# Prompt attention of an encoder step: the head outputs' squares on ScalarE instead of GpSimd, each head's store and every second copy of weights issued earlier

## The reference, cut to what matters

```python
def diff_attn_prompt(q, k, v, lam):          # q, k: (1, 1024, 8, 2, 64), v: (1, 1024, 8, 128)
    for i in range(T // Q_BLOCK):            # blocks of 128 queries
        qs, qe = i * Q_BLOCK, (i + 1) * Q_BLOCK
        s = jnp.einsum('bqhcd,bkhcd->bhcqk', q[:, qs:qe], k[:, :qe])
        mask = chunk_id[None, :qe] <= chunk_id[qs:qe, None]
        p = jax.nn.softmax(jnp.where(mask, s, -jnp.inf), axis=-1)
        a = p[:, :, 0] - lam * p[:, :, 1]
        outs.append(jnp.einsum('bhqk,bkhv->bqhv', a, v[:, :qe]))

def diff_output(o, g_norm, lambda_init, w_o):
    o = rms_norm(o, g_norm) * (1.0 - lambda_init)     # per head, over its 128 columns
    return o.reshape(B, T, DIFF_V) @ w_o
```

## Time and profile before

| what | value |
|---|---|
| median of 3 runs | 2890.35 us (2889.14 to 2894.65) |
| the profiled execution | 2889.26 us, its span 2886.80 us |
| PE / DVE / ACT / POOL busy in the span | 2791.4 / 1168.9 / 866.4 / 1236.5 us |
| prompt attention within the span | about 1680 to 1892 us |
| mean granted clock of PE over the span | 0.989 |

### The profile page before, as it was taken

How to read it: one execution, slowest core, us unless ns; L and a number is a source line. 1 busy time by engine, 2 the same in 40 slices (tenths; PEclk the granted TensorE clock), 3 DMA queues, 4 the chain that set the end, 5 groups by cost and what they waited for, 6 DMA issues and landing times.

```text
span 2886.8 us, 39210 instructions
## 1 busy us (share of the span) xinstructions
PE 2791.4 (97%) x15484; PEld 2420.7 (84%) x15484; DVE 1168.9 (40%) x2079; ACT 866.4 (30%) x1513; POOL 1236.5 (43%) x654
## 2 busy tenths in 40 slices
PE   7999999999999999999999988899999999999997
PEld 7977757799889988997788867777798899989986
DVE  2153156452322233246544178855463322232245
ACT  2053242231222223222211056653141222222221
POOL 1211210343776567634212122133252775677645
PEclk9999999999999999999999999999999999999999
DMA  4111216110210221031444333476111201221021
GB/s 134 52 37 44 91 64 226 37 52 30 59 36 22 58 58 44 15 95 37 128 135 143 123 134 107 168 291 236 44 53 36 55 8 54 58 58 31 27 73 66
DMA packets 197372, 232.26 MB, mean 80 GB/s; under 512 B 8944, under 2 KB 141808, under 8 KB 195200
## 3 DMA queue, kind: packets, MB, share of 16 engines
q1 hardware_dynamic: 197248, 230.54, 24.8%
HBM read 184.90 MB, written 45.61 MB: 80 GB/s over the span
## 4 chain that ended last, share of the span: by engine, by line
PE 44%; DVE 4%; issue 1%; DMA 1%; ACT 1%; POOL 0%; SPq 0%; DVEq 0%; ACTq 0%
PE ps L1480 13%; PE ps L1498 12%; PE ps L1781 8%; PE ps L1668 3%; DVE stats L2513 1%; PE ps L1884 1%; PE ps L1751 1%; PE ps L1847 1%; PE ps L1918 1%; DMA o_scr<-oraw 1%; PE ps L1871 1%; PE ps L1470 1%; DVE stats L2226 1%; PE ps L1962 1%; ACT PR L1360 0%
## 5 line engine op out<-in xcount | busy, mean ns | idle before, releaser
L1480 PE MATMUL ps<-xt,wsplit 128*128 128x384 f32 x5184 | 908.2, 335 | 13.1 <-DVEq L2253 5.0
L1480 PEld LDWEIGHTS ps<-xt,wsplit 128*128 128x128 f32 x5184 | 900.8, 188 | 17.9 <-issue 7.1
L852 POOL TENSOR_TENSOR wsplit<-raw,wsplit 128x1024 fp32r<-128x1024 f32 x144 | 354.7, 2470 | 920.8 <-ACT wsplit L1072 843.1
L1498 PE MATMUL ps<-wsplit,xt 128*128 128x512 f32 x3024 | 707.0, 393 | 0.0
L1498 PEld LDWEIGHTS ps<-wsplit,xt 128*128 128x128 f32 x3024 | 564.8, 189 | 122.0 <-issue 6.5
L1781 PE MATMUL ps<-wsplit,HF 128*128 128x512 f32 x2016 | 468.6, 390 | 0.0
L1781 PEld LDWEIGHTS ps<-wsplit,HF 128*128 128x128 f32 x2016 | 377.3, 188 | 81.6 <-DVE x_res L2359 4.2
L2359 DVE TENSOR_TENSOR x_res<-x_res,ps 128x1024 f32<-128x1024 f32 x168 | 205.2, 1221 | 308.3 <-PE ps L1781 308.3
L2351 DVE TENSOR_SCALAR Hf<-ps 128x384 f32<-128x384 f32 x144 | 80.3, 558 | 499.1 <-PE ps L1480 498.4
L1278 ACT ACTIVATE Hf<-Hf 128x384 f32<-128x384 f32 x144 | 75.9, 527 | 428.1 <-DVE Hf L2351 428.1
L922 POOL TENSOR_TENSOR wsplit<-raw,wsplit 128x1024 fp32r<-128x1024 f32 x36 | 86.0, 2389 | 263.9 <-ACT wsplit L1255 263.9
(11 more groups left out here) (196 smaller groups left out, 2782.8 us busy)
## 6 DMA issues: line engine op xcount, KB each, us to landing
raw<-in_w_up SPq DMA_DIRECT2D x64, 512.0 KB, 5.5
raw<-in_w_down SPq DMA_DIRECT2D x64, 512.0 KB, 3.7
kq_scr<-kqst SPq DMA_DIRECT2D x64, 256.0 KB, 2.8
Kc<-in_cache_k SPq DMA_DIRECT2D x8, 2048.0 KB, 13.3
Vc<-in_cache_v SPq DMA_DIRECT2D x8, 2048.0 KB, 8.8
raw<-in_w_in_a SPq DMA_DIRECT2D x24, 512.0 KB, 3.7
out<-kvs SPq DMA_DIRECT2D x36, 256.0 KB, 2.2
raw<-in_w_kv SPq DMA_DIRECT2D x16, 512.0 KB, 4.4
```

Source lines behind the costliest of these rows:

```text
L852: nc.gpsimd.tensor_tensor(wsplit[:, slot, 1, :], raw[:, slot, :], wsplit[:, slot, 0, :].bitcast(F32), ALU.subtract).then_inc(lo_done, 1)
L1480: last = nc.tensor.matmul(ps[0:M, b, 0:GW], st, xt[:, c, k, ng * GW:(ng + 1) * GW], start=(k == 0 and i == 0), stop=(k == KT - 1 and i == 2))
L1498: last = nc.tensor.matmul(ps[:, u % 6, :], xt[:, a, 2 * j + k, tok:tok + P], wsplit[:, (g + j) % 4, c, k * 512:(k + 1) * 512], start=(j == ...
```

## The change

Four edits. ACT squares each head output in the step after its copy: one activation Square of 128x128 with its accumulator, which writes the sum of the row to `ssA` (`output_squares`); it stands after the second exponential of the loop's turn. POOL's `head_squares` is gone; its remaining waits on it are waits on ACT's count. SP issues `head_out(k - 1)` at step 4 of head k, ahead of that step's `head`, and no longer at step 7 behind `values_in`. DVE copies the far weights (`rest_weights`) ahead of `balance` instead of behind it.

```diff
@@ SP: the loop over the steps
         for s in range(STEPS):
+            if s % PT == 4 and s // PT:
+                head_out(s // PT - 1)
             if s % PT == 4 and s // PT + 2 < H_B:
                 head(s // PT + 2)
             if s % PT == PT - 1 and s // PT + 3 < H_B:
                 values_in(s // PT + 3)
-            if s % PT == PT - 1 and s // PT:
-                head_out(s // PT - 1)
@@ POOL
-        def head_squares(h):
-
-            pool.wait_ge(o_free, PT * (h + 1))
-            tt(osq[:], oraw[h % 2][:], oraw[h % 2][:], ALU.mult).then_inc(heads_squared, 1)
-            pool.wait_ge(heads_squared, h + 1)
-            for k, half in enumerate((64, 32, 16, 8, 4, 2, 1)):
-                to = osq[:, :, 0:half] if half > 1 else ssA[:, PT * h:PT * (h + 1)].unsqueeze(2)
-                tt(to, osq[:, :, 0:half], osq[:, :, half:2 * half], ALU.add).then_inc(heads_summed, 1)
-                pool.wait_ge(heads_summed, 7 * h + k + 1)
-
         for j in range(4):
             split_lo(G_O2 + j)
-        for h in range(H_B - 1):
-            head_squares(h)
+        pool.wait_ge(heads_squared, PT * (H_B - 1))
...
-        head_squares(H_B - 1)
+        pool.wait_ge(heads_squared, STEPS)
         nc.gpsimd.memset(Vc[:, 1, 4, :], 0.0).then_inc(smp_v_zero, 1)
@@ ACT
             if s % PT == 0 and h >= 2:
                 act.wait_ge(o_out[h % 2], 16 * (h // 2))
-                act.wait_ge(heads_squared, h - 1)
             nc.scalar.activation(oraw[h % 2][:, i, :], ps[:, 7, 0:P], ACT.Copy).then_inc(o_free, 1)
+
+        def output_squares(s):
+            h, i = step_of(s)
+            act.wait_ge(o_free, s + 1)
+            if s:
+                act.wait_ge(heads_squared, s)
+            nc.scalar.activation(osq[:, 0, :], oraw[h % 2][:, i, :], ACT.Square,
+                                 accum_out=ssA[:, step_index(s):step_index(s) + 1]).then_inc(heads_squared, 1)
...
             if s + 1 < STEPS:
                 exponentials(s + 1, 1)
+            if 0 <= s - 3:
+                output_squares(s - 3)
@@ DVE
             if s + 1 < STEPS:
                 maxima(s + 1)
-            if 0 <= s < STEPS:
-                balance(s)
             if 0 <= s - 1 and s % 2 == 1:
                 rest_weights(s - 1)
             if 0 <= s < STEPS:
+                balance(s)
                 combine(s)
...
-            dve.wait_ge(heads_summed, 7 * H_B)
+            dve.wait_ge(heads_squared, STEPS)
```

More of the change, by code:

```diff
@@ L307, in encoder_step @@
     heads_squared = sem("heads_squared")
-    heads_summed = sem("heads_summed")
     factor_made = sem("factor_made")
```

## The result

The changed kernel took 2870.41 us (median of 4 runs, 2868.65 to 2872.81) against 2889.74 us, ratio 0.9931 with a 95% interval of 0.9914 to 0.9948: 19.3 us less, where 2869 us, or 21.4 us less than the first median, was forecast. The profiled execution took 2868.72 us, its span 2866.6.

The account below looks back on a forecast made before the run. PE and DVE were taken to share the bound in an undisturbed prompt-attention head, with late stores stalling later heads. -18.6 + 0 - 2.4 = -21.0 us took the profiled 2889.26 to 2868.3, so 2869 us was forecast, range 2862 to 2881.

Parts of the forecast that it names:

- Stores sooner: Prompt attention, SP's queue: earlier head stores end ACT's wait at oraw and the lower clock, -18.6 us.
- Squares on ACT: Prompt attention, 64 steps: a 0.31 us square each fits ACT's idle time ahead of lead copies; 0, up to +5 us.
- upper bound of 5 us: Squares on ACT: cost if the 0.31 us slip stayed in two of eight steps a head, 16 x 0.31.
- POOL off and far weights sooner: Prompt attention, DVE: POOL's squares leave, far copy precedes balance; -2.4 us net, from -8 to +4.
- POOL's 0.59 us a head: DVE's factor product and combination, stretched beside POOL, shorten once POOL's squares leave; 4.7 us in eight heads.
- DVE's new wait: DVE would idle 0.6 us at the early far copy for PE's far transposes; with combination lags, up to 1.1 us a head.
- The seam to the sample stage: Second load of cached values loses its 1.9 us wait for POOL's zeroing, but off the chain: 0.
- (a): DVE becomes the bound in order, far copies waiting for PE in all 32 odd steps: +23.4 us, 2895 us; chance 0.06.
- (b): ACT becomes the bound, all 64 squares on the path: +19.8 us, 2889 us, no change; chance 0.06.
- (c): The wait only moves to another late thing at a head's start; half of 18.6 us comes back, 2881 us; chance 0.06.
- (d): PE becomes the only bound, every head falling to its 21.95 us: 2863 us; chance 0.12.
- The sum: Whole kernel: -18.6 + 0 - 2.4 = -21.0 us, giving 2868.3 us for the profiled execution, 2869 us forecast.

Follow-up runs that it names:

- e1: Kernel before with only the stores early (each head's store issued at step 4 of the next head): 2873.4 us, ratio 0.9945.
- e4: Changed kernel with the stores put back late, behind the values load at each head's last step: 2886.2 us, ratio to before 0.9987.
- e5: Changed kernel with every square done twice on ACT, the second into spare columns: 2868.1 us (one run).
- e6: Changed kernel with no squares of prompt head outputs on any engine, their sums set to one: 2873.5 us (one run).
- e2: Changed kernel with the copy of the far weights put back behind balance on DVE: 2872.8 us.
- e3: Changed kernel with the squares and sums back on POOL and none on ACT, stores and far copy as changed: 2875.2 us.
- e7: Changed kernel with balance ahead of the far copy again in one odd step of each head: 2869.1 us, ratio to before 0.9939.
- e8: e7 with the maxima of both maps as one reduction instead of two in a head's four small steps: 2868.6 us, ratio to before 0.9938.
- e10: Changed kernel with one more small DVE instruction, a second reciprocal, in every step: 2876.1 us (one run).

## Why the prediction was right, point by point

- **Stores sooner, -18.6 us: right.** e1 gives 18.63 us over the six heads from this edit alone. The reading that named the cause was the code's wait beside ACT's unexplained idle time, and e4's trace names the store outright. Taking the price from the periods and not from ACT's 15.6 us of idle time was right as well. But the working put the difference of 3 us down to the clock alone, and that it is so small is luck: a stall without the echo costs some 0.6 us less than ACT's idle time and one with it 0.9 us more (the last section has the rows), so that by an estimate from these the echo made some 6 of the 18.6 us. (The stall at 1770.30 us, whose windows show, is the second, not the third.)
- **Squares on ACT, 0: right**, and with more room than I saw. The square takes 0.32 us, and e5 and e6 leave the head where it is. The upper bound of 5 us is excluded. The sign given for it, that the idle time ahead of the lead copies falls by about 20 us, came true (21.6 us), but only some 12 us of that are the squares.
- **POOL off and far weights sooner, -2.4 us net: right in the sum, wrong in its parts.** Six heads gained 137.93 - 135.60 = 2.3 us here, 0.39 a head, where 0.3 was taken. But the working added POOL's 0.59 us a head, the earlier copy and DVE's new wait as separate terms. The step that failed is the first: in the order of before, POOL's removal together with the squares on ACT gives 0.06 us a head (e1 to e2), since a part of the stretch stood in a wait for PE and no engine waited for the rest. And the earlier copy by itself, with POOL at work, would have cost 0.44 us a head (e1 to e3). Only both together give 0.39. The idle time that I foresaw at this step did come, 0.55 us in each head for 0.6 forecast; what it costs stays open, since e7 only moved it. Head 0, which the working counted among eight, gained nothing (26.10 us before, 26.25 after).
- **The seam to the sample stage, 0: right.** From the opening reduction of head 7 to the first read-back of attended outputs on the chain it is 1973.06 - 1862.44 = 110.6 us before and 1951.58 - 1841.27 = 110.3 us after.
- **The rivals.** (a), DVE in order as the bound, is nearest to e3, where it would have cost 0.44 us a head, not the 2.9 it would need. (b) is excluded by e5, (c) by e1. (d), PE's floor of 21.95 us, is approached but not reached, also by e7 and e8.
- **The sum** of -21.0 us held to the last MLP (21.9); 1.7 us were lost behind it, about what the ten products fewer in the ten microseconds at 0.83 come to, and the medians differ by 19.3.

## What to carry to other kernels

When an engine sits idle with no releaser named, read the semaphores of its line in the code: here it was a store queued on SP behind a load that waited for a later event, and moving one line of the issue order gave nine tenths of the gain. Price a stall from the period of a repetition that runs without it, not from the idle time. And don't add up the prices of two edits at one wait: work that stands ahead of a wait for another engine can be covered by it, and the same work behind it costs what some other engine then waits for. When an added or moved instruction is to measure a price, read in the trace what it did add before dividing by it.

## What the runs showed of the hardware

A stall costs more than its length only where the clock falls behind it. The first two stalls of the kernel before, by ACT's wait at the copy into oraw, and their heads:

```profile
1745.33 0.28 ACT L1377 ACTIVATE oraw<-ps 128x128 f32<-128x128 f32 x1 [2.50 <-issue]
1770.30 0.28 ACT L1377 ACTIVATE oraw<-ps 128x128 f32<-128x128 f32 x1 [2.67 <-issue]
```

```profile
1728.87:1753.69 24.82, 22.24 (x197) 18.58 (x198) 21.88 (x44) 17.50 (x48) 5.52 (x8) 1.00 0.36 129
1753.69:1780.25 26.56, 23.82 (x197) 20.14 (x198) 21.93 (x45) 17.42 (x48) 5.51 (x8) 0.94 0.34 119
```

At a clock of 1.00 a wait of 2.50 us cost 1.83 us over the 22.99 of head 1; with the clock at 0.94 one of 2.67 us cost 3.57. The three later stalls of this kernel, all at 0.94, cost 0.9 us more than their wait each; in e4 the first three, at 1.00, cost 0.5 to 0.6 us less than theirs (2.25 to 2.63 us). Why the clock fell behind some stalls and not behind others of the same kind, these runs don't show. And at one place of the program far from any change, the execution of the changed kernel ran ten microseconds at 0.83 where that of the kernel before ran at 1.00; the start of the attention stage itself moved between 1678.1 us (e4) and 1684.6 us (e10) with nothing changed ahead of it.
